# A hybrid attention step with a gathered expert layer on one core: the second head is chosen ahead of the first dot, query blocks take other ring places and come sooner, the late strips begin two slots later

## The chip, the core and the metric

The kernel runs on one core of a Trainium2 chip. The metric is the device time of one execution in microseconds, as the median of several runs. The engines are PE (TensorE), VectorE (DVE), ScalarE (ACT), GpSimd (POOL) and SyncE (SP); the core has 16 DMA engines, which all queues share.

## The reference

One layer of a decoder runs over 256 prompt tokens and 32 sample tokens (8 sequences of 4, each with 2048 cached positions). All is float32, the model width is 2048.

```python
h = layer_norm(ALPHA * x + mix @ w_out, ln1_g, ln1_b)           # mix: stick-breaking heads | sparse attention heads
return layer_norm(ALPHA * h + peer_ffn(h, ...), ln2_g, ln2_b)

# peer_ffn, for each block of tokens xc
q = (xc @ w_query).reshape(128, 8, 2, 128)
s = jnp.einsum('thcd,ckd->thck', q, sub_keys)
top_s, top_i = lax.top_k(s, 16)                                  # 16 best of 128 sub-keys, on both sides
cand_s, cand_i = 16 x 16 sums and expert numbers
best_s, best_j = lax.top_k(cand_s, 16)
experts = jnp.take_along_axis(cand_i, best_j, axis=-1)           # 8 heads x 16 experts for each token
gate = jax.nn.softmax(best_s, axis=-1)
act = jax.nn.gelu(jnp.einsum('thkd,td->thk', u_tab[experts], xc))
return jnp.einsum('thk,thkd->td', gate * act, v_tab[experts])
```

Ahead of it stand one input projection, stick-breaking attention over prompt and cache, and the sparse attention (compressed keys, selected blocks, a window) over prompt and cache.

## The kernel before, in words

**Stages.** The input projection and the attention of the prompt's early rows come first, with 1 MB blocks of weights and cache pages streamed through a ring. Then the output projection for the first 160 tokens (128 "full rows", tile 0, and 32 rows, tile 1), their layer norm, the query projection and the choice of experts. From there on a long loop of 288 slots gathers expert rows, while the attention of the samples and of the last prompt rows, with all that follows for the last 128 tokens, runs in the loop's background.

**The ring.** `Stream` (L276) numbers the 1 MB items that SyncE loads and gives each one of 8 ring places (`RING`, 8192 bytes a partition each). `room` is how many items must be used before a place is free again; PE raises `item_used` by one with the last matmul on each item. The 16 blocks of `w_out` ("output blocks", key `wo`) lie in places 4 to 7 and 0 to 3 in turn, twice; the 16 blocks of `w_query` ("query blocks", key `wq`) take place k modulo 4. Places 4 to 7 (`u_ring`) are left to the gathers of `peer_u`, places 0 to 3 (`v_ring`) go to those of `peer_v` once all items are used (`stream.n`).

**Order on PE** (L1588 to L1669). For output blocks 0 to 7 both tiles' passes follow block by block; for 8 to 15 the full rows of all eight come first, and only then the 32-row passes (`out_rows(k, 1)`), each of which ends its block's use. Then the first two query blocks' full rows (their use doesn't end there), the turned rows of tile 1, `query_parts` for blocks 0 to 2, which end their use, and blocks 3 to 15 (`query_rows`), one after another, each followed by the scores of the one before.

**Order on SyncE** (L687 to L729). The output blocks, `w1_one` (one side of the compression weights), the query blocks in order, then the background's items (`Background`): pages of the compressed caches in places of another set (`later_rows`, four areas of 2048 words from `AT_T` on, of which the first pages use the third and fourth). The page numbers are read into registers ahead of each set of pages. ScalarE issues the odd pages from the third set on.

**Order on VectorE** (L2746 to L2762). Rows of tile 0 and 1 are normed, then the first head of tile 0 is chosen: `head_part` 0 and 1 take the 16 best sub-keys on each side, part 2 the 16 best pairs; `first_ranks` and `second_ranks` make expert numbers, `fold` lays them out by slot. `chosen` tells GpSimd. Then comes the slot loop. A slot `s` runs `selection(s)` (parts of other heads by tables of slot numbers: `HEAD_PARTS`, `EXPERT_PARTS`, `EXPERT_HEADS`), `background(s)` and `gather_dot(s)`: it waits for gathered rows in ring place 4 + s % 4 and multiplies and sums 128 x 2048 values in one instruction.

**Order on GpSimd** (L2815 to L2859). It waits for the first `chosen` and for the ring, then issues in each step `s` the gather of `peer_u` for slot s (when the dot of slot s - 4 is done) and, from s = 19 on, that of `peer_v` for slot s - 19. `CHOSEN_BY` says which slots wait for a further head.

**Late strips.** Six units of the prompt's sparse attention (`LATE`) run in the loop. A unit that begins at slot or tick L has scores on PE at L, `strip_mask` on VectorE at L + 1, exponentials on ScalarE at L + 2, `strip_norm` at L + 3, PE's transposes at L + 4 (`LATE_TURN`), the values on PE at L + 5 (`LATE_PV`) and the result's copy at L + 6. `strip_cmp_in` copies the transposed compressed probabilities; VectorE runs it at the end of slot L + 4, and PE's values wait for it.

Of the kernel before, what the change touches and what calls it, by code (L numbers as in the profile page):

```python
# [145 lines left out]
RING = 8  # L146
# [11 lines left out]
LATE_AT, LATE_STEP = 14, 6  # L158
# [116 lines left out]

class Stream(Items):  # L276


    def __init__(self):
        super().__init__(RING)  # L280
        order = []
        for step, m in enumerate(ORDER):
            order.append((("w_in", m), 1))
            for name, at in (("ak", AK_AT), ("av", AV_AT)):
                if step in at:
                    order += [((name, at[step], b4), 2) for b4 in range(4)]
        order += [(("av", i, b4), 2) for i in range(8, 16) for b4 in range(4)]
        order += [(("wo", k), 1) for k in range(16)]
        for key, dmas in order:
            self.add(key, self.n % RING, dmas)  # L290
        for k in range(16):
            self.add(("wq", k), k % 4, 1)
# [71 lines left out]
def hybrid_step(nc, dram, outs):  # L364
    stream, later_items = Stream(), Background()
    with ExitStack() as ctx:
# [45 lines left out]
        ring = [words(AT_RING + 2048 * s, 2048) for s in range(RING)]  # L412
# [26 lines left out]
        ring_full = [sem(f"ring_full{s}") for s in range(RING)]  # L439
# [197 lines left out]
        HEAD_PARTS = {part: (0, 1, part) for part in range(3)}  # L637
        HEAD_PARTS.update({4 + 3 * k + part: (0, 2 + k, part) for k in range(2) for part in range(3)})
# [5 lines left out]
        EXPERT_PARTS = {10: (0, 1, 0), 11: (0, 1, 1), 27: (0, 2, 0), 28: (0, 2, 1), 43: (0, 3, 0), 44: (0, 3, 1)}  # L644
        EXPERT_PARTS.update({91 + 8 * p + part: (1, p, part) for p in range(4) for part in range(2)})
        EXPERT_PARTS.update({QUERY_AT + 10 + 12 * p + part: (2, p, part) for p in range(1, 4) for part in range(2)})
        EXPERT_HEADS = {3: (0, 1), QUERY_AT + 6: (2, 0), QUERY_AT + 10: (2, 1)}
# [24 lines left out]
        def _(sp):  # L672
# [40 lines left out]
            for k in range(16):  # L713
                load(("wq", k), dram["w_query"][k].rearrange("p k n -> p (k n)"))
# [17 lines left out]
            sp.wait_ge(h_in, 5)  # L732
            for kv in range(2):
# [1247 lines left out]
        def _(dve):  # L1981
# [497 lines left out]
            def experts_head(tt, h):  # L2479
                first_ranks(tt, h, 1)  # L2480
                second_ranks(tt, h, 1)
# [144 lines left out]
            def background(s):  # L2626
                if s in LATE_OUT:
                    strip_out(LATE_OUT[s])
                if s in LATE_MASK:
# [118 lines left out]
            experts_head(0, 0)  # L2748
            dve.wait_ge(saved, 1)

            for s in range(SLOTS_ALL):
                selection(s)
# [6 lines left out]
                if s in LATE_TURN:  # L2759
                    strip_cmp_in(LATE_TURN[s])  # L2760
# [20 lines left out]
        def _(pool):  # L2781
# [34 lines left out]
            pool.wait_ge(item_used, stream.used["wo", 15])  # L2816
# [95 lines left out]
```

## Time and profile before

| | before |
|---|---|
| median of 3 runs | 2444.26 us (2441.86 to 2447.72) |
| the profiled execution's own time | 2442.06 us |
| its span, first to last instruction | 2440.3 us |
| PE busy | 1744.5 us (71%) |
| VectorE busy | 1281.0 us (52%) |
| GpSimd busy | 842.5 us (35%) |
| moved by DMA | 961.28 MB, mean 394 GB/s |
| mean granted TensorE clock | 0.801 of full speed |

The span is what the profile's rows are about; the own time holds a little around it. Busy shares are means over stages with different limits. The page's second part shows the span in 40 slices of 61 us each, as tenths of busy time. The stretches and rows of single engines that matter lie between 586 and 760 us, at the turn from the output projection to the slot loop.

### The profile page before, as it was taken

To read this page: it belongs to the slowest core of one execution; us is meant where nothing else is said; L and a number is where in the kernel's file an instruction comes from. 1 tells how busy PE (TensorE), PEld (TensorE's weight loads), DVE (VectorE), ACT (ScalarE), POOL (GpSimd) and SP (SyncE) were. 2 spreads that over 40 slices of the span, in tenths; PEclk is the share of its full clock that TensorE was granted. 3 is DMA by queue.
4 is the path that set the end of the run, shared out by engine and by line. 5 is a ranking of instruction groups with operands and counts; after the bars stand their busy time and mean duration, and the time that the engine had idled before them with its cause. 6 is when DMAs were issued, how large, how long until landed. Compare 5 with 4: busy or idle time off the path is not lost.

```text
span 2440.3 us, 30172 instructions
## 1 busy us (share of the span) xinstructions
PE 1744.5 (71%) x9939; PEld 967.4 (40%) x9939; DVE 1281.0 (52%) x2454; ACT 354.1 (15%) x817; POOL 842.5 (35%) x595
## 2 busy tenths in 40 slices
PE   8999999989989877887565756869433333355335
PEld 6777766643887655565312222228100000000000
DVE  0600112362797877557958452245788754455651
ACT  0001101330411111111100020022200010021111
POOL 0000000000123434343323242242665677767662
PEclk9999999999999988889787878979555555555556
DMA  9989999998699999999999999999999999999998
GB/s 386 374 343 362 369 386 374 367 387 333 280 377 384 406 407 409 407 407 406 398 390 396 390 402 407 419 421 421 419 422 412 422 422 421 422 421 422 422 422 324
DMA packets 213309, 961.28 MB, mean 394 GB/s; under 512 B 23841, under 2 KB 89378, under 8 KB 122754
## 3 DMA queue, kind: packets, MB, share of 16 engines
q0 software_dynamic: 84432, 626.31, 62.4%
q1 hardware_dynamic: 92914, 300.39, 31.8%
q10 hardware_dynamic: 35808, 32.65, 4.0%
q8 instruction: 80, 1.31, 0.2%
q14 instruction: 75, 0.61, 0.1%
HBM read 952.77 MB, written 14.88 MB: 397 GB/s over the span
## 4 chain that ended last, share of the span: by engine, by line
DMA 43%; PE 41%; DVE 6%; ACTq 4%; issue 4%; POOL 1%; ACT 1%; SPq 0%; POOLq 0%; DVEq 0%
DMA sb<-in_peer_v,sb 23%; PE bank L1197 14%; DMA sb<-in_nsa_t 13%; PE bank L1677 6%; DMA sb<-in_peer_u,sb 4%; PE bank L1960 4%; PE bank L1563 3%; PE bank L1610 3%; PE bank L1268 2%; DVE sb L2706 2%; ACTq L455 2%; DMA sb<-in_nsa_v 2%; PE bank L1296 2%; ACTq L1034 1%; PE bank L1875 1%
## 5 line engine op out<-in xcount | busy, mean ns | idle before, releaser
L2706 DVE CUSTOM_DVE_ANT_0 sb<-sb 128x2048 f32<-128x2048 f32 x288 | 659.5, 2293 | 448.8 <-DMA sb<-in_peer_u,sb 443.4
L1960 PE MATMUL bank<-sb 128*32 128x512 f32 x2304 | 466.9, 861 | 495.8 <-DMA sb<-in_peer_v,sb 459.4
L2819 POOL DMA_INDIRECT sb<-in_peer_v,sb x288 | 503.9, 1749 | 525.3 <-PE bank L1960 476.5
L2819 POOL DMA_INDIRECT sb<-in_peer_u,sb x288 | 330.2, 1147 | 491.7 <-DVE sb L2706 287.8
L1960 PEld LDWEIGHTS bank<-sb 128*32 128x32 f32 x2304 | 60.8, 126 | 806.1 <-DMA sb<-in_peer_v,sb 730.0
L1197 PE MATMUL bank<-sb 128*128 128x288 f32 x1408 | 352.1, 410 | 7.7 <-DMA sb<-in_tokens_t 7.7
L1677 PE MATMUL bank<-sb 128*128 128x256 f32 x1024 | 275.3, 428 | 84.1 <-DMA sb<-in_nsa_t 72.1
L1197 PEld LDWEIGHTS bank<-sb 128*128 128x128 f32 x1408 | 266.1, 191 | 92.7 <-issue 13.9
L1677 PEld LDWEIGHTS bank<-sb 128*128 128x128 f32 x1024 | 247.0, 309 | 123.3 <-DMA sb<-in_nsa_t 85.1
L1154 ACT ACTIVATE sb<-sb 128x32 f32<-128x32 f32 x288 | 87.4, 316 | 720.1 <-PE bank L1960 433.9
L2803 POOL DMA_DIRECT2D out_a<-sb x1 | 0.5, 547 | 501.7 <-PE bank L1296 501.7
L1743 PE MATMUL bank<-sb 128*32 128x512 f32 x128 | 66.1, 692 | 43.0 <-DMA sb<-in_nsa_t 43.0
L1797 PE MATMUL bank<-sb 128*32 128x256 f32 x256 | 62.5, 426 | 30.7 <-DMA sb<-in_nsa_v 30.7
L779 ACT ACTIVATE sb<-bank 128x288 f32<-128x288 f32 x44 | 18.1, 411 | 410.1 <-PE bank L1197 410.1
L962 ACT ACTIVATE sb<-sb 32x2048 f32<-32x2048 f32 x36 | 68.6, 1906 | 39.7 <-issue 26.2
L1563 PE MATMUL bank<-sb 128*32 128x512 f32 (+1 forms) x256 | 71.8, 599 | 0.1
L1610 PE MATMUL bank<-sb 128*128 128x160 f32 (+1 forms) x512 | 71.0, 297 | 0.7 <-ACT sb L935 0.7
L1610 PEld LDWEIGHTS bank<-sb 128*128 128x128 f32 x512 | 67.7, 190 | 3.3 <-ACT sb L975 2.0
L1296 PE MATMUL bank<-sb 128*32 128x512 f32 x512 | 60.9, 597 | 5.1 <-DMA sb<-in_a_v 5.0
L1875 PE MATMUL bank<-sb 128*128 128x128 f32 x512 | 61.0, 279 | 3.4 <-DMA sb<-in_w_query 3.4
L1875 PEld LDWEIGHTS bank<-sb 128*128 128x128 f32 x512 | 58.7, 194 | 11.7 <-DMA sb<-in_w_query 7.5
L1268 PE MATMUL bank<-sb 128*32 128x256 f32 x1024 | 58.6, 380 | 0.0
(412 smaller groups left out, 1448.7 us busy)
## 6 DMA issues: line engine op xcount, KB each, us to landing
sb<-in_a_k SPq DMA_DIRECT2D x128, 512.0 KB, 7.3
sb<-in_a_v SPq DMA_DIRECT2D x128, 512.0 KB, 6.8
sb<-in_w_in SPq DMA_DIRECT2D x43, 1024.0 KB, 9.2
sb<-in_w_out SPq DMA_DIRECT2D x32, 1024.0 KB, 19.3
sb<-in_w_query SPq DMA_DIRECT2D x32, 1024.0 KB, 9.7
sb<-in_nsa_t SPq DMA_DIRECT2D x200, 128.0 KB
sb<-in_nsa_t ACTq DMA_DIRECT2D x184, 128.0 KB
sb<-in_nsa_v SPq DMA_DIRECT2D x64, 128.0 KB
```

Of the source, the lines that this page charges most:

```text
L962: act.activation(replica(g)[32 * q:32 * q + 32], src, ACT.Copy).then_inc(rep_in, 1)
L1154: act.activation(diag[j % 4], const["fold"], ACT.Copy, scale=w16[:, r % 2, j:j + 1]).then_inc(diag_in, 1)
L1197: mm = pe.matmul(bank[step % 2][:, 0:T], w[:, kt * P:(kt + 1) * P], x_t[:, kt, :], start=(kt == 0), stop=(kt == KT - 1))
L1268: mm = pe.matmul(bank[4 + u % 2][32 * b4:32 * b4 + 32, 256 * pp:256 * pp + 256], q_pad_a[:, half, b4, h], rows[b4][:, :, h, :], start=(h = ...
L1296: mm = pe.matmul(bank[(0 if half else 6) + c][r, :], z_t[:, half, 2 * pp + j, r], rows[b4][:, 1024 * j + 512 * c:1024 * j + 512 * c + 512] ...
L1563: mm = pe.matmul(bank[3 * (n % 2) + tt][own, :], mix(4 * kq + kt)[:, P * tt:P * tt + rows], w[:, kt, :], start=(kq == 0 and kt < parts), s ...
L1610: mm = pe.matmul(bank[5 if m == 1 else 1 if m == 2 else m % 2][:, 0:count], w[:, P * kt:P * kt + P], h_t[:, kt, 0:count], start=(kt == 0), ...
L1677: mm = pe.matmul(bank[(7, 3)[n % 2]][:, 0:256], rows[:, :, l], w1_one[:, :, l, :], start=(l == 0), stop=(l == 15), skip_group_check=True)
L1875: mm = pe.matmul(bank[2 + m % 2][:, 0:ROWS_2], w[:, P * kt:P * kt + P], h_t2[:, kt, :], start=(kt == 0), stop=(kt == KT - 1))
L1960: mm = pe.matmul(bank[g % 2][32 * c:32 * c + 32, :], diag[j % 4], rows[:, 512 * c:512 * c + 512], start=(s in FIRST), stop=(s in LAST), sk ...
L2706: dve.tensor_tensor_reduce(out=u, in0=u, in1=replica(g), scale=1.0, scalar=0.0, op0=ALU.mult, op1=ALU.add, accum_out=act16[:, r % 2, j:j + ...
L2819: pool.indirect_dma_start(rows[j % 4], None, dram[table], bass.IndirectOffsetOnAxis(ap=idx, axis=0)).then_inc(full[j % 4], 16)
```

## The change

- The set of ring places grows by a ninth, `words(AT_T + 4096, 2048)`. It is the area that the third set of the background's places uses later.
- Query blocks take places by a table: 0 to 2 in places 4 to 6, 3 to 6 in 0 to 3, block 7 in the ninth, then 0, 1, 2, 3, ninth, 0, 1, 2. SyncE issues block 7 ahead of block 0.
- Before the first pages SyncE waits until query block 12 is used. GpSimd waits for query block 2 in place of output block 15 before its first gather.
- The second head of tile 0 is chosen (three parts and its first ranks) ahead of the loop. Its second ranks and folds are at slot 1 in a new function. Heads 2 and 3 and the pair's expert numbers move two slots forward.
- The late strips begin at 16 in place of 14, and `strip_cmp_in` moves from the end of slot L + 4 to the background of slot L + 5.

```diff
-LATE_AT, LATE_STEP = 14, 6
+LATE_AT, LATE_STEP = 16, 6
+WQ_AT = (4, 5, 6, 0, 1, 2, 3, 8, 0, 1, 2, 3, 8, 0, 1, 2)
...
         for k in range(16):
-            self.add(("wq", k), k % 4, 1)
+            self.add(("wq", k), WQ_AT[k], 1)
...
-        ring = [words(AT_RING + 2048 * s, 2048) for s in range(RING)]
+        ring = [words(AT_RING + 2048 * s, 2048) for s in range(RING)] + [words(AT_T + 4096, 2048)]
...
-        HEAD_PARTS = {part: (0, 1, part) for part in range(3)}
-        HEAD_PARTS.update({4 + 3 * k + part: (0, 2 + k, part) for k in range(2) for part in range(3)})
+        HEAD_PARTS = {2 + 3 * k + part: (0, 2 + k, part) for k in range(2) for part in range(3)}
...
-        EXPERT_PARTS = {10: (0, 1, 0), 11: (0, 1, 1), 27: (0, 2, 0), 28: (0, 2, 1), 43: (0, 3, 0), 44: (0, 3, 1)}
+        EXPERT_PARTS = {8: (0, 1, 0), 9: (0, 1, 1), 27: (0, 2, 0), 28: (0, 2, 1), 43: (0, 3, 0), 44: (0, 3, 1)}
...
-        EXPERT_HEADS = {3: (0, 1), QUERY_AT + 6: (2, 0), QUERY_AT + 10: (2, 1)}
+        EXPERT_HEADS = {QUERY_AT + 6: (2, 0), QUERY_AT + 10: (2, 1)}
...
-            for k in range(16):
+            for k in (7, *range(7), *range(8, 16)):
                 load(("wq", k), dram["w_query"][k].rearrange("p k n -> p (k n)"))
...
             sp.wait_ge(h_in, 5)
+            sp.wait_ge(item_used, stream.used["wq", 12])
...
             def experts_head(tt, h):
                 first_ranks(tt, h, 1)
+                experts_told(tt, h)
+
+            def experts_told(tt, h):
                 second_ranks(tt, h, 1)
...
             def background(s):
                 if s in LATE_OUT:
                     strip_out(LATE_OUT[s])
+                if s in LATE_PV:
+                    strip_cmp_in(LATE_PV[s])
...
             experts_head(0, 0)
+            for part in range(3):
+                head_part(0, 1, part)
+            first_ranks(0, 1, 1)
             dve.wait_ge(saved, 1)

             for s in range(SLOTS_ALL):
+                if s == 1:
+                    experts_told(0, 1)
                 selection(s)
...
                 gather_dot(s)
-                if s in LATE_TURN:
-                    strip_cmp_in(LATE_TURN[s])
...
             pool.wait_ge(chosen, 1)
-            pool.wait_ge(item_used, stream.used["wo", 15])
+            pool.wait_ge(item_used, stream.used["wq", 2])
```

## Rows read from the trace of the kernel before

**Rows 1.** The page: mean busy share of the DMA engines, 40 slices, in tenths.

```profile
DMA  9989999998699999999999999999999999999998
```

**Rows 2.** Busy time by stretch: bounds and length, engines, granted clock, DMA share, GB/s.

```profile
598.00:619.00 21.00, 21.00 (x86) 8.38 (x88) 5.08 (x10) 2.30 (x3) 0.00 (x0) 1.00 0.01 4
619.00:630.00 11.00, 9.92 (x88) 7.90 (x81) 10.48 (x24) 4.26 (x6) 0.00 (x0) 1.00 0.95 379
630.00:640.00 10.00, 9.37 (x147) 8.84 (x149) 9.01 (x30) 6.29 (x12) 0.00 (x0) 1.00 0.09 14
640.00:646.00 6.00, 6.00 (x65) 5.80 (x58) 5.00 (x22) 2.88 (x4) 0.26 (x1) 1.00 0.91 365
646.00:714.00 68.00, 67.34 (x462) 62.74 (x463) 56.48 (x144) 22.46 (x49) 14.06 (x15) 1.00 1.02 413
714.00:719.00 5.00, 5.00 (x24) 5.00 (x24) 5.00 (x5) 0.38 (x1) 3.04 (x2) 1.00 0.30 80
768.00:775.00 7.00, 7.00 (x36) 5.93 (x35) 6.65 (x16) 0.38 (x1) 2.70 (x3) 1.00 0.88 297
720.00:1520.00 800.00, 575.51 (x2859) 361.56 (x2858) 536.83 (x1069) 102.36 (x283) 289.19 (x233) 0.85 1.03 401
1520.00:2400.00 880.00, 446.30 (x2424) 120.39 (x2424) 499.10 (x832) 119.09 (x268) 520.92 (x322) 0.60 1.01 419
```

**Rows 3.** SyncE's queue in order of time: start, length, line, what, number.

```profile
586.83 0.37 SPq L712 DMA_DIRECT2D sb<-in_cmp_w  x1
618.49 2.90 SPq L687 DMA_DIRECT2D sb<-in_w_query  x4
638.94 6.81 SPq L687 DMA_DIRECT2D sb<-in_w_query  x4
687.17 0.33 SPq L687 DMA_DIRECT2D sb<-in_w_query  x1
692.14 3.96 SPq L725 DMA_DIRECT2D sb<-in_nsa_t  x8
700.71 3.46 SPq L725 DMA_DIRECT2D sb<-in_nsa_t  x6
```

**Rows 4.** PE in order of time, and SyncE's waits from 598 to 720.

```profile
620.93 1.09 PE L1578 MATMUL bank<-sb 128*128 128x128 f32 x8
640.88 4.51 PE L1610 MATMUL bank<-sb 128*128 128x160 f32 x32
709.51 11.02 PE L1677 MATMUL bank<-sb 128*128 128x256 f32 x48 [0.66 <-ACT sb L967]
...
SPq L687 <- PE bank L1563: 32.8, 4, 31.3
```

**Rows 5.** VectorE in order of time; brackets: idle before, and its releaser.

```profile
614.10 0.69 DVE L2341 SCALAR_TENSOR_TENSOR sb<-sb,bank 128x512 f32<-128x512 f32 x1 [13.04 <-PE bank L1563]
633.00 0.30 DVE L2399 MAX8 sb<-sb 128x8 f32<-128x128 f32 x1
639.65 0.15 DVE L2422 COPY sb<-sb 128x1 f32<-128x1 f32 x1
642.48 0.43 DVE L2440 TENSOR_TENSOR sb<-sb 128x256 f32<-128x256 f32 x1
655.68 2.29 DVE L2706 CUSTOM_DVE_ANT_0 sb<-sb 128x2048 f32<-128x2048 f32 x1 [7.98 <-DMA sb<-in_peer_u,sb]
714.76 2.29 DVE L2706 CUSTOM_DVE_ANT_0 sb<-sb 128x2048 f32<-128x2048 f32 x1
751.38 0.28 DVE L2178 COPY sb<-bank 15x128 f32<-15x128 f32 x1 [8.18 <-PE bank L1396]
```

**Rows 6.** GpSimd in order of time.

```profile
645.74 1.00 POOL L2819 DMA_INDIRECT sb<-in_peer_u,sb  x1 [82.06 <-DVEq L2486]
715.65 2.21 POOL L2819 DMA_INDIRECT sb<-in_peer_u,sb  x1 [5.43 <-DVE sb L2706]
759.08 0.94 POOL L2819 DMA_INDIRECT sb<-in_peer_u,sb  x1 [12.59 <-DVE sb L2706]
```

More of the change, by code:

```diff
@@ L273, in add @@
         self.used[key] = self.n
+WQ_AT = (4, 5, 6, 0, 1, 2, 3, 8, 0, 1, 2, 3, 8, 0, 1, 2)
 class Stream(Items):
     def __init__(self):
-        super().__init__(RING)
+        super().__init__(RING + 1)
         order = []
@@ L438, in hybrid_step @@
         item_used = sem("item_used")
-        ring_full = [sem(f"ring_full{s}") for s in range(RING)]
+        ring_full = [sem(f"ring_full{s}") for s in range(RING + 1)]
         consts_in, first_in, x_in, wg_in, rope_in, w1_in, pages_in = (sem(n) for n in (
```

## The prediction

> **What bounds the kernel now.** I read the page first: the DMA row of its 40 slices is at 9 nearly everywhere and falls to 6 in one slice, the eleventh (610 to 671 us) [rows 1]. The reader is to see that a full row of DMA engines is the limit, and that the kernel gets shorter only where they stand still. So I went to the busy time by stretch for the DMA share [rows 2]. From 720 us on it is 1.01 over two long stretches, with one small dip (0.88 over 7 us at 768). Between 598 and 719 it has three holes. A: share 0.01 over 21 us and 0.95 over the next 11, together 20.8 + 0.5 = 21.3 us. B: 0.09 over 10 us and 0.91 over 6, together 9.1 + 0.5 = 9.6 us. C: 0.30 over 5 us, 3.5 us. With the dip D (0.12 x 7 = 0.8 us) that is 35.2 us. Both sides of the change read and write the same bytes, so the time gained is the idle time of the DMA engines taken away, less what is added.
>
> Then the queues around these holes. SyncE issues the slab of compression weights at 586.83, and next query block 0 at 618.49; blocks 4 to 7 go out from 638.94 [rows 3]. SyncE's waits put this down to PE's output-projection line, 31.3 us the longest: block 0 waits for the ring place of output block 12 [rows 4]. VectorE works without a gap from 614.10 to the end of the first head's selection; GpSimd's first gather is at 645.74, released by it [rows 5, 6]. One 1 MB item takes 1.0486 MB / 413 GB/s = 2.54 us of all engines, from the stretch 646 to 714 [rows 2].
>
> **Hole A.** Query block 7 gets a ring place of its own (behind the ring, where neither the slab of compression weights nor the norms lie), no wait, and is issued first, right behind 586.83: one item, 2.5 us, moves into the hole. Blocks 0 to 2 go to places 4 to 6, so block 0 waits for output block 8 instead of 12. The one-row passes of blocks 8 to 15 lie between VectorE's row at 614.10 (which the last full-row pass releases, some 0.2 us before) and PE's next line at 620.93: 7.0 us for eight, 0.88 each [rows 4, 5]. Four of them earlier is 3.5 us: issue at 618.49 - 3.5 = 615.0. The blocks behind it (places of blocks 12 to 15) are issued between 618.5 and 621.2 as now, while the first three keep the engines busy 7.6 us: no gap. A shrinks by 2.5 + 3.5 = 6.0 us.
>
> **Hole B.** Seven blocks (0 to 6) then run from about 615.9 (the issue and the 0.9 us that the engines took after 618.49 to be busy in the stretches) to 615.9 + 7 x 2.54 = 633.7. The next work is block 8, which waits for block 3's place (now the fourth issue of the row at 638.94, about 645.4), and the first gather. Neither comes earlier: VectorE's chain from 614.10 has no wait on the moved transfers, it ends at 645.7 as now, and GpSimd's new wait (query block 2 used, instead of output block 15) is met before 640.88, when PE is past those parts [rows 4]. So the engines stand from 633.7 to about 646.4: 12.7 us instead of 9.6, 3.1 us lost. If the first gather or block 8 came 1 us later, B grows by 1 us. A and B together give 2.9 us.
>
> **The first slots.** Now VectorE waits 7.98 us for the first gathered rows, until 655.68, since they queue with blocks 4 to 7 [rows 5]. After, the queue is empty at 645.7, so the rows land within two or three items (some 5 to 7 us), by about 652. What takes VectorE's wait in exchange is its own work: the second head's three parts and its first ranks are put there. From the first head's rows, 633.00 to 639.65 is 6.65 us and to 642.48 another 2.83, together 9.5 us [rows 5], so the first dot starts at 645.7 + 9.5 = 655.2 instead of 655.7: which costs nothing. Slots 0 to 3 are rid of 6.65 + 2.83 us less the first part (about 1.8): 7.7 us of lead. The rest of that head (3.2 us: 642.48 to 645.7) stays, at slot 1. The pair's ranks move from slots 10, 11 to 8, 9, behind heads 2 and 3, which begin two slots sooner.
>
> **Hole C.** It is there because no gather is out: GpSimd idles 5.43 us before 715.65, for a dot that stands behind the pair's ranks at slot 11, and the page loads wait for PE's taps at 709.51 (released at 717) [rows 4, 6]. With the lead, the dot of slot 11 ends near 707.5, and five dots of 2.29 us follow one another [rows 5]: the gathers 15 to 18 come between 707 and 715. The ledger from 646.4: 8 query blocks, gathers 0 to 14 and 2 MB of pages are 25 items, 63.5 us, to 709.9; gathers 15 to 18 to 720; by then the next pages (717.2 as now) and gather 19 with the first value gather are there. C goes: +3.5 us. Worth between 0 (hole moved, not closed) and 3.5; I take 3.5 because each demand in the ledger is issued before its turn.
>
> **The waits on SyncE.** The first page load now waits for query block 12 used. PE's blocks of 5.1 us (640.88 to 709.51 less the scores' end, 13 blocks) make that 640.9 + 10 x 5.1 = 692; today the last query block goes out at 687.17 and, after eight page numbers are read, the first page at 692.14 [rows 3]. So the first pages start at 692 + 5.0 = 697, the second set at 705.5 instead of 700.71, done issuing near 710. Behind the waiting instruction stand only these pages. PE wants the first set at 709.51 and the second at half of its 11 us row, near 717: the first set has 8 us after its last issue, the second 7, for 2 to 3 items. Cost 0; if the margin fails, its lower bound is 0 and its upper the 4.8 us shift itself.
>
> **The late strips.** The strips start at slots 16, 22, ... instead of 14, 20, ..., and the copy of the turned probabilities moves from the end of a slot to the next one, behind its selection. Today that copy makes VectorE wait 8.18 us (751.38), GpSimd has no gather for 12.59 us, and the dip D, 0.8 us, follows [rows 2, 5, 6]. Moving it can return 0.8. Against it: the mask of the first strip now waits for scores that stand on PE behind the third set of pages' taps, so VectorE may wait at slot 17 instead. Bounds: +0.8 and, one such stall with two gathers (5.1 us) out, about -4. I take 0, nearest to D's row. The strips' ends at slot 52 have the output projection far behind them.
>
> **A rule weighed.** The gather issued at 715.65 took 2.21 us where others took 1.00 [rows 6]; the dot that began at 714.76 ended at 717.05, the next came at once [rows 5]. The Trainium skill, "SBUF — State Buffer", section "Who interferes with whom", says that a VectorE instruction with two inputs in SBUF and a GpSimd instruction that reads SBUF exclude each other, the loser blocked for the whole instruction. By that rule, the trace agrees. It speaks against this change, since it makes five dots in a row where the gathers are needed; its time is the third case below, worked out from the rows.
>
> **Sum.** 6.0 - 3.1 + 3.5 + 0 = 6.4 us. The profiled execution took 2442.06 us, its span 2440.3: 2442.06 - 6.4 = 2435.7. The median is 2.2 above the profiled one, and a median is what is forecast: 2444.26 - 6.4 = **2437.9 us**. A difference under 0.2% (4.9 us: below 2439.4, above 2449.1) can't be told from none.
>
> **Cases.**
> 1. As summed, 2437.9, own range 2434 to 2441: chance 0.50, of which 0.06 lies within 0.2%.
> 2. Only A and B count: the lead in dots is spent, since slot 16 waits for PE's turn at 725 anyway, and hole C comes back between 722 and 745. Gain 2.9, 2441.4. For it: PE's chain to 709.51 is untouched; against: the value gathers can start with slot 15. Chance 0.20, nearly all within 0.2%.
> 3. Gathers shut out by dots: one gather per dot, each a dot late. The first of the row then misses its turn by 2.3 us: 2440.2. Chance 0.08, within.
> 4. The strips' move also returns D, and waits for the strips elsewhere in VectorE's first 50 slots shorten: gain 7.2 to 10, 2435.5. Chance 0.10, faster.
> 5. Slower: the strips' waits. At slot 17 the mask, and again at the next unit, and the one after, holds VectorE as long as the copy did (8.2 us), now with only 5.1 us of gathers out. Each empties the queue for about 5 us (8.2 and a slot's own 2.3 less 5.1); three are 15 lost against 6.4: 2444.3 + 8.6 = 2452.9. It makes the kernel slower from the second stall on, and measurably from the third. For it: one stall of 8.18 is there now; against: it cost but 0.8. Chance 0.12.
>
> Faster by over 0.2%: 0.44 + 0.10 + 0.03 of case 2 = 0.57; within: 0.06 + 0.17 + 0.08 = 0.31; slower: 0.12. The range goes from case 4's better end, 2434.3, less the 2.4 us by which a run shown lies under the median, to 2446, one hole of case 5 beyond case 1 and the scatter (2437.9 + 5 + 3).
>
> **What would show it.** Query block 0 issued near 615, one block right behind 586.8; DMA idle from about 601 to 616 and 634 to 646, and a share of 1 from 646 through 725; first dot near 655; slot 11's dot over before 709; first pages at 697; PE's taps still at 709.5. Wrong if: the first gather comes later than 646.5, a hole of over 2 us opens between 690 and 760, VectorE waits over 8 us at a strip's mask, or PE waits for the first pages.

## The result and the profile after

| | before | after |
|---|---|---|
| median on one chip, 11 runs each | 2445.17 us (2441.86 to 2448.36) | 2451.53 us (2447.3 to 2455.63) |
| ratio after / before | | 1.0020, 95% interval 1.0011 to 1.0029 |
| the profiled execution, own time and span | 2442.06 and 2440.3 us | 2449.86 and 2448.1 us |
| mean granted TensorE clock | 0.801 | 0.795 |

The change makes the kernel slower by 0.2% (0.0020 of 2445.17 is 4.9 us; the plain medians lie 6.4 apart). Forecast were 2437.9 us and a gain of 6.4.

After, busy time by stretch, in the columns of [rows 2] (length; PE, PEld, VectorE, ScalarE and GpSimd busy; granted clock; DMA share; GB/s):

```profile
598.00:619.00 21.00, 21.00 (x83) 8.42 (x85) 4.68 (x10) 2.30 (x3) 0.00 (x0) 1.00 0.25 97
619.00:630.00 11.00, 9.92 (x88) 7.63 (x81) 10.52 (x23) 4.18 (x6) 0.00 (x0) 1.00 0.99 416
630.00:640.00 10.00, 9.37 (x138) 8.84 (x141) 9.05 (x29) 6.29 (x13) 0.00 (x0) 1.00 0.47 195
640.00:646.00 6.00, 6.00 (x79) 5.80 (x67) 5.15 (x23) 2.83 (x5) 0.00 (x0) 1.00 0.00 0
646.00:714.00 68.00, 67.34 (x464) 62.76 (x464) 62.06 (x150) 22.57 (x50) 19.85 (x18) 1.00 0.96 381
714.00:719.00 5.00, 3.39 (x16) 3.09 (x14) 3.96 (x11) 0.38 (x1) 1.62 (x2) 1.00 1.02 415
733.00:747.00 14.00, 13.53 (x66) 13.18 (x66) 5.71 (x15) 0.98 (x3) 1.87 (x2) 1.00 0.39 110
720.00:1520.00 800.00, 583.84 (x2842) 366.21 (x2843) 524.22 (x1044) 101.23 (x279) 289.80 (x227) 0.84 1.01 394
```

A is 21 x 0.75 + 11 x 0.01 = 15.9 us (forecast 15.3, before 21.3). B is 10 x 0.53 + 6 = 11.3 us (forecast 12.7, before 9.6). C is full: 1.02 where [rows 2] has 0.30. But two things stand where nothing was forecast. One is a new hole, 0.39 from 733 to 747, 8.5 us. The other is the stretch from 646 to 714, at 0.96 after 1.02 of [rows 2]. In parts, with 1.02, 1.02 and 1.05 for the same three before:

```profile
646.00:660.00 14.00, 14.00 (x101) 12.99 (x101) 12.76 (x45) 8.27 (x14) 5.01 (x5) 1.00 0.93 376
690.00:703.00 13.00, 13.00 (x94) 12.24 (x93) 12.04 (x31) 1.81 (x7) 2.00 (x2) 1.00 0.92 350
703.00:709.00 6.00, 6.00 (x43) 5.36 (x42) 6.00 (x5) 1.47 (x6) 4.82 (x3) 1.00 0.76 242
```

One us each is missing right behind the first gather and from 690 to 703 (the pages start at 697 and not at 692), and 1.4 us from 703 to 709. The view of the DMA queues from 702 to 710, 40 slices of 0.2 us, shows the last one:

```profile
DMA  8979999999999910000000993663989898999959
```

The engines are dry from 705.0 to 706.4: it is hole C, 10 us sooner and less than half as long. GpSimd's gather beside the dots in a row takes 2.21 us there, as in [rows 6] (703.57 below).

SyncE's queue after, as [rows 3]:

```profile
587.23 0.37 SPq L714 DMA_DIRECT2D sb<-in_cmp_w  x1
...
697.30 4.30 SPq L727 DMA_DIRECT2D sb<-in_nsa_t  x8
706.20 3.94 SPq L727 DMA_DIRECT2D sb<-in_nsa_t  x8
```

The two sets of pages are issued where the prediction put them (697 and 705.5, done near 710). PE after, in order of time, as [rows 4]. These matmuls multiply the pages with the compression weights (the prediction's "taps"), 32 for each set of 8 pages; brackets hold the idle time before:

```profile
709.92 7.47 PE L1680 MATMUL bank<-sb 128*128 128x256 f32 x32 [0.66 <-ACT sb L970]
727.44 6.00 PE L1680 MATMUL bank<-sb 128*128 128x256 f32 x16 [10.05 <-DMA sb<-in_nsa_t]
```

This is the failure. Before, the row at 709.51 has 48 matmuls without a stop. Now PE does the first set's 32 and stands 10.05 us for the second set, whose last issue ended at 706.20 + 3.94 = 710.14: 17 us from last issue to use. VectorE and GpSimd after, as [rows 5, 6]; dots stand for rows between:

```profile
655.68 2.29 DVE L2714 CUSTOM_DVE_ANT_0 sb<-sb 128x2048 f32<-128x2048 f32 x1
...
738.83 0.48 DVE L2527 TENSOR_SCALAR sb<-bank,sb 128x256 f32<-128x256 f32 x1 [16.50 <-PE bank L1692]
```

```profile
646.13 0.99 POOL L2830 DMA_INDIRECT sb<-in_peer_u,sb  x1 [82.22 <-DVEq L2492]
...
703.57 2.21 POOL L2830 DMA_INDIRECT sb<-in_peer_u,sb  x1 [5.43 <-DVE sb L2714]
...
710.51 0.94 POOL L2830 DMA_INDIRECT sb<-in_peer_u,sb  x1 [0.30 <-issue]
...
743.70 0.94 POOL L2830 DMA_INDIRECT sb<-in_peer_u,sb  x1 [19.01 <-DVE sb L2714]
```

Read these as a chain. The gathers have their lead: the one of slot 16 comes at 710.51, and in the kernel before at 718.17, 7.66 us later (forecast were 7.7 us of lead). Then VectorE waits 16.50 us for PE's taps, no dot runs, no ring place comes free, and GpSimd issues nothing for 19.01 us. The DMA engines have nothing left, and the hole at 733 opens.

### The profile page after: what moved, and what is told of

It is laid out like the page before. It is cut to its first block, busy times and chain, and to the rows that moved or that the text cites. A ratio compares the mean times of both kernels' runs of the same rounds, so it can differ in the third digit from the quotient of the medians.

```text
span 2448.1 us, 30172 instructions
## 1 busy us (share of the span) xinstructions
PE 1756.8 (72%) x9939; PEld 971.4 (40%) x9939; DVE 1280.5 (52%) x2454; ACT 353.9 (14%) x817; POOL 851.8 (35%) x595
## 4 chain that ended last, share of the span: by engine, by line
DMA 43%; PE 38%; DVE 7%; issue 5%; ACTq 3%; POOL 1%; SPq 1%; ACT 1%; POOLq 0%; DVEq 0%
DMA sb<-in_peer_v,sb 25%; PE bank L1200 14%; DMA sb<-in_nsa_t 9%; DMA sb<-in_peer_u,sb 5%; PE bank L1680 4%; PE bank L1963 4%; PE bank L1566 3%; DVE sb L2714 3%; PE bank L1271 2%; PE bank L1613 2%; DMA sb<-in_nsa_v 2%; PE bank L1299 2%; ACTq L458 2%; POOL sb L2830 1%; DMA sb<-in_w_out 1%
## 5 line engine op out<-in xcount | busy, mean ns | idle before, releaser
L1963 PE MATMUL bank<-sb 128*32 128x512 f32 x2304 | 468.7, 862 | 485.3 <-DMA sb<-in_peer_v,sb 455.5
L2830 POOL DMA_INDIRECT sb<-in_peer_u,sb x288 | 340.6, 1183 | 488.9 <-DVE sb L2714 284.5
L1746 PE MATMUL bank<-sb 128*32 128x512 f32 x128 | 70.7, 738 | 42.7 <-DMA sb<-in_nsa_t 42.7
L1800 PE MATMUL bank<-sb 128*32 128x256 f32 x256 | 63.6, 435 | 32.4 <-DMA sb<-in_nsa_v 32.4
L1299 PE MATMUL bank<-sb 128*32 128x512 f32 x512 | 60.9, 598 | 5.3 <-DMA sb<-in_a_v 5.3
L1839 PE MATMUL bank<-sb 128*32 128x512 f32 x512 | 59.3, 608 | 4.0 <-DMA sb<-in_w_out 4.0
```

The source lines that it names most:

```text
L1299: mm = pe.matmul(bank[(0 if half else 6) + c][r, :], z_t[:, half, 2 * pp + j, r], rows[b4][:, 1024 * j + 512 * c:1024 * j + 512 * c + 512] ...
L1746: mm = pe.matmul(bank[((5, 6), (7, 2))[ph][c]][32 * b4:32 * b4 + 32, :], q_pad[:, 4 * h + b4, g], rows[:, 4 * c:4 * c + 4, g, :], start=(g ...
L1963: mm = pe.matmul(bank[g % 2][32 * c:32 * c + 32, :], diag[j % 4], rows[:, 512 * c:512 * c + 512], start=(s in FIRST), stop=(s in LAST), sk ...
L2830: pool.indirect_dma_start(rows[j % 4], None, dram[table], bass.IndirectOffsetOnAxis(ap=idx, axis=0)).then_inc(full[j % 4], 16)
```

## Why the pages were late: packets, not items

The view of the DMA queues by stretch gives the packets, MB and share of each queue: q0 is GpSimd's (gathers), q1 SyncE's, q10 ScalarE's. Before, from 706 to 709:

```profile
q1 hardware_dynamic: 626, 0.57, 57.7%
q0 software_dynamic: 76, 0.62, 51.6%
```

After, from 715 to 718 and from 727 to 730:

```profile
q0 software_dynamic: 150, 1.10, 88.0%
q1 hardware_dynamic: 148, 0.14, 13.3%
...
q0 software_dynamic: 117, 0.96, 78.3%
q1 hardware_dynamic: 120, 0.11, 11.2%
q10 hardware_dynamic: 117, 0.11, 10.3%
```

From 715 to 718, where both queues have work, each moves the same number of packets (150 and 148), and with three queues too (117, 120, 117). A gather's packets are 7.3 KB in the mean (1.10 MB / 150), a page's 0.9 KB (0.14 MB / 148); the rows are 8 and 1 KB, and the count holds some packets under 512 B. So a page queue beside waiting gathers gets 1/9 of the bytes, 0.14 MB in 3 us, and a set of 1 MB would take 22 us. Before, GpSimd idled 5.22 us for want of a dot just ahead of this gather, and 5.43 us ahead of the next [rows 6]:

```profile
709.15 1.07 POOL L2819 DMA_INDIRECT sb<-in_peer_u,sb  x1 [5.22 <-DVE sb L2706]
```

So few gathers were out, 76 of their packets went by from 706 to 709, and the pages got 0.57 MB in these 3 us. Hole C itself let no page through: the second set's last packets moved by 713, and the view by queue has none of SyncE's from 713 to 718. What let the pages through were the same pauses of GpSimd for want of a dot of which hole C is the last. The Trainium skill, "DMA: Bandwidth & Descriptors", section "Queues, rings and completion order", says that each DMA engine goes round the queues that have work and changes only at a packet's end. By that rule, the trace agrees: 150 against 148.

## Experiments

Each was run beside the kernel before on the same chip, but not all on one chip; the kernel before had medians of 2445.72, 2446.71, 2445.82 and 2446.59 us beside them. So kernels are compared by their ratios to it, given with a 95% interval, and not by their medians.

| kernel | median, us | ratio | interval |
|---|---|---|---|
| strips_old | 2452.79 | 1.0028 | 1.0016 to 1.0039 |
| the changed kernel | 2451.53 | 1.0020 | 1.0011 to 1.0029 |
| head_wait_b | 2448.86 | 1.0010 | 0.9998 to 1.0023 |
| gathers_held | 2448.75 | 1.0009 | 0.9998 to 1.0019 |
| strips_only | 2445.85 | 0.9997 | 0.9988 to 1.0007 |
| split_pages_b | 2443.66 | 0.9997 | 0.9983 to 1.0012 |
| ring_once | 2445.22 | 0.9995 | 0.9985 to 1.0004 |
| before_wait | 2446.25 | 0.9994 | 0.9983 to 1.0005 |
| ring_wait_b | 2443.83 | 0.9993 | 0.9982 to 1.0003 |
| ninth_once | 2445.37 | 0.9989 | 0.9978 to 1.0000 |
| head_only | 2444.19 | 0.9988 | 0.9978 to 0.9998 |
| split_same_time | 2441.33 | 0.9984 | 0.9973 to 0.9995 |
| ninth_strips_old | 2442.00 | 0.9983 | 0.9973 to 0.9992 |
| scores_first_b | 2440.27 | 0.9975 | 0.9962 to 0.9988 |
| scores_split | 2440.39 | 0.9974 | 0.9965 to 0.9984 |

**ninth_once: the changed kernel, the ninth place used once, so that SyncE waits for block 7 only.**

```diff
-WQ_AT = (4, 5, 6, 0, 1, 2, 3, 8, 0, 1, 2, 3, 8, 0, 1, 2)
+WQ_AT = (4, 5, 6, 0, 1, 2, 3, 8, 0, 1, 2, 3, 0, 1, 2, 3)
-            sp.wait_ge(item_used, stream.used["wq", 12])
+            sp.wait_ge(item_used, stream.used["wq", 7])
```

> The changed kernel, with the ninth place used for query block 7 alone (places 4, 5, 6, 0, 1, 2, 3, 9th, 0, 1, 2, 3, 0, 1, 2, 3), so that SyncE waits for block 7 in place of block 12 and the first pages are issued near 692 again, as in the kernel before (697.30 in the changed one). Theory 1 (the second set of pages, issued at 706.2, shared the DMA engines packet by packet with a burst of gathers, 1 KB against 8 KB, landed 17 us after its last issue, and PE's wait of 10.05 us for it stopped VectorE for 16.50 us and GpSimd for 19.01): the sets are issued before the burst, PE waits under 2 us for pages between 709 and 730, the DMA hole from 733 to 747 (about 8 us idle) is gone, and the median falls by 7 to 10 us under the changed kernel, to 2441 to 2445. Theory 2 (the move of the late strips, with the other waits only following from it): no change beyond 2 us, 2450 to 2453. Theory 3 (the gathers' lead itself is what PE pays for, whenever pages are issued): PE still waits over 5 us, 2448 or more.

The pages start at 693.19, and the loss is gone: 0.9989 against 1.0020, apart by 0.0031 (with the two half-widths of the intervals taken together, 0.0009 and 0.0011, by 0.0017 to 0.0045). One thing more comes with this edit: with the ninth place used once, the last query block waits for a later place, and SyncE issues its last one at about 688 and not at 682. So head_wait_b below, where the wait stands without the ring's part, is needed too. The second set is in time, the third isn't:

```profile
732.93 9.36 PE L1680 MATMUL bank<-sb 128*128 128x256 f32 x32 [6.12 <-DMA sb<-in_nsa_t]
```

**strips_old: the changed kernel, with the late strips as before.**

```diff
-LATE_AT, LATE_STEP = 16, 6
+LATE_AT, LATE_STEP = 14, 6
-                if s in LATE_PV:
-                    strip_cmp_in(LATE_PV[s])
+                if s in LATE_TURN:
+                    strip_cmp_in(LATE_TURN[s])
```

> The changed kernel with the late strips alone put back: first at slot 14, and the copy of the turned probabilities at the end of slot L + 4. Theory 1 (late pages): the hole from 733 to 747 stays, PE's wait for pages at 717 to 727 stays near 10 us, the median stays within 3 us of the changed kernel's 2451.5, on either side, since the first strip's scores come ahead of the wait and its copy may stop VectorE again. Theory 2 (the strips' move is the loss): the median falls by 6 us or more, to 2445 or less.

It takes nothing of the loss away (1.0028). PE waits 6.56 us for the second set, VectorE 16.4 at the first mask, GpSimd 21.86: the strips' move isn't the cause, and with late pages the old order is no better.

**before_wait: the kernel before with SyncE's wait for query block 12 alone.**

```diff
             sp.wait_ge(h_in, 5)
+            sp.wait_ge(item_used, stream.used["wq", 12])
```

> The kernel before with one line added: SyncE waits until query block 12 is used before the first pages. Theory 1: the first pages are issued 5 us later (697 in place of 692), the second set at 706. VectorE is where it was, so the gathers 15 to 18 come only from 715 on, and hole C (share 0.30 from 714 to 719) is there for the pages: they land by about 718, PE waits 0 to 3 us for them, and the median is 0 to 3 us above 2445.2. A theory that the wait alone is the loss: PE waits about 5 us or more and the median is 5 us or more above.

0.9994: pages 4 us later cost nothing by themselves. The first starts at 696.09; PE waits 2.65 and 2.97 us where [rows 4] stands.

**gathers_held: the changed kernel; GpSimd waits for the second set before the gather of slot 15.**

```diff
             (GpSimd's loop)
+                if s == 15:
+                    pool.wait_ge(later_full[3], 128)
```

> The changed kernel with one wait more on GpSimd: gather 15 and those behind it are held until the second set of pages has landed. If pages and gathers share the engines by packets (theory 1), the set that is issued by 710 lands by about 713 instead of 727, PE's wait at 717 is gone, VectorE's 16.50 us at the sums are gone, and the DMA hole at 733 to 747 with them, against a hole of up to 3 us near 710 and dots a few us later: median 4 to 8 us under the changed kernel, 2443 to 2448. If the set was late for its own issue or for a slow path of its own, it lands no earlier than 720 and the median stays at 2451 or above.

With the gathers out of the way the second set lands by 716.7, 10 us sooner, and PE's row has its 48 matmuls again. Its PE and GpSimd:

```profile
710.00 11.02 PE L1680 MATMUL bank<-sb 128*128 128x256 f32 x48 [0.66 <-ACT sb L970]
```

```profile
716.74 0.94 POOL L2830 DMA_INDIRECT sb<-in_peer_u,sb  x1 [8.62 <-DVE sb L2714]
751.93 0.94 POOL L2830 DMA_INDIRECT sb<-in_peer_u,sb  x1 [18.44 <-DVE sb L2714]
```

So gathers are what delays the pages. But the third set then meets the gathers: PE waits 9.60 us for it at 735.90, VectorE 14.86 us at the mask, and GpSimd's gap (18.44) is as long as in the changed kernel (19.01), only later. The hole was expected to go and the median to reach 2443 to 2448; neither came. How much of the loss stays isn't told: 1.0009 is clearly apart neither from the changed kernel nor from the one before.

**ninth_strips_old: ninth_once and strips_old together.** Its diff is the two above.

> The changed kernel with the ninth place used once (block 7) and the late strips back at 14 with the old copy: the first two parts of the change alone, with early pages. With the ninth place used once, PE still waited 6.12 us for the third set of pages, and VectorE 10.46 us at the first strip's mask, whose scores stand behind that set's taps. Theory 1 (each wait is for pages behind gathers, and the mask only passes it on): with scores at 14 the mask is not stopped, VectorE waits under 3 us there, though some of it comes back at the copy of slot 18; the median is 1 to 4 us under that kernel's 2445.4, 2441.5 to 2444.5. Theory 2 (the strips' place is neutral here too, since the whole is bound by DMA afterwards): within 1 us, 2444.5 to 2446.5.

0.9983, faster than the kernel before. From ninth_once it can't be told (0.9989); here the mask waits 7.55 us and GpSimd 12.59.

**ring_once, head_only, strips_only: the kernel before with one part of the change each** (ring and query blocks with the ninth place used once, SyncE's order of blocks and GpSimd's wait as changed; the second head's choice ahead of the first dot, with the tables of slots as changed; the strips' move). Each is shortened to its main lines:

```diff
ring_once:   +WQ_AT = (4, 5, 6, 0, 1, 2, 3, 8, 0, 1, 2, 3, 0, 1, 2, 3)
             +sp.wait_ge(item_used, stream.used["wq", 7])
head_only:   +head_part(0, 1, 0..2); first_ranks(0, 1, 1)   ahead of the slot loop
strips_only: -LATE_AT = 14   +LATE_AT = 16, strip_cmp_in in background(L + 5)
```

> The kernel before with the places and the order of the query blocks alone (the ninth place used once, pages issued near 692). Holes A and B by the prediction's sum are 2.9 us less. Theory 1 (a lead of the dots over PE's pages is given back in waits): the first gathered rows land early, VectorE's wait of 7.98 us shrinks to about 3 us, its dots are 4 to 5 us ahead, and the burst of gathers falls on the second and third set; the gain of 2.9 is kept in part, 2443 to 2446. A theory that the ring part is simply good and the head the spoiler: 2440 to 2443.

> The kernel before with the second head chosen ahead of the first dot and heads 2, 3 and the pair two slots earlier, nothing else. The first gathered rows land at 655.7 as before, and the head takes 9.5 us from 645.7, so the first dot is at 655.7; the dots lead by 7 to 8 us at slot 16 as in the changed kernel, and gathers 14 to 18 come between 703 and 715, while pages are issued at 692 and 700. Theory 1: pages of the third set wait behind the gathers, hole C (3.5 us) closes at 714 but one of 3 to 5 us opens between 733 and 750; median 2444 to 2448. If a lead of the dots is worth what it closes: 2441 to 2443.

> The kernel before with the late strips two slots later and the copy in the next slot, nothing else. Theory 1 (the strips only pass on waits for pages): VectorE's wait of 8.18 us at the copy goes, a wait of 2 to 8 us comes at the first mask (slot 17), the dip of 0.8 us at 768 goes; median within 2 us of 2445.7. Theory 2 (the strips are the loss): 5 us or more above.

The head's move is worth a little alone (0.9988), the ring's part and the strips' can't be told from nothing. In head_only the first dot is at 657.59, since the gathers queue with query blocks; in ring_once it is at 654.84, 6.19 us waited. In head_wait_b below, whose code is the same as head_only's up to there, it is at 655.90 with no wait, so these small waits differ between executions, and the ring's part isn't needed for a start without one.

strips_only missed its expectation on the waits (2 to 8 us at the first mask): its mask waits 13.52 us, PE 9.19 us for the third set, and GpSimd has a gap of 17.11 us, nearly that of the changed kernel. Its ratio is 0.9997 all the same. So a long gap in one profile doesn't by itself show a loss in the median. The profiled execution was the slowest of its eleven (2448.87 us).

**head_wait_b and ring_wait_b: the wait for block 12 with the head's move, and with the ring's part.**

```diff
head_wait_b: head_only   +sp.wait_ge(item_used, stream.used["wq", 12])
ring_wait_b: ring_once   -WQ_AT = (..., 8, 0, 1, 2, 3, 0, 1, 2, 3)
                         +WQ_AT = (..., 8, 0, 1, 2, 3, 8, 0, 1, 2)
                         -sp.wait_ge(item_used, stream.used["wq", 7])
                         +sp.wait_ge(item_used, stream.used["wq", 12])
```

> The kernel before with two things alone: the second head chosen ahead of the first dot, and SyncE's wait for query block 12 ahead of the pages. Ring and strips as before. Theory, that the loss comes from the two together (gathers come earlier, pages later, and pages asked for behind gathers get about a ninth of the bytes): the second set of pages lands late, TensorE waits 5 to 10 us for it at the taps, VectorE behind it, and GpSimd has a gap of over 14 us between 720 and 760; median 3 to 8 us above that of the head move alone, which was 2444.2, so 2447 to 2452. Rival, that the ring's part is needed too: no more than 2 us above the head move alone, 2443 to 2446.

> The kernel before with the ring's part alone, exactly as changed (ninth place used twice, so SyncE's wait for block 12 stands ahead of the pages); head and strips as before. Theory, that wait and lead must meet: the first dot stays near 655, the gathers have no lead, so the pages meet fewer gathers; median within 3 us of the ring part with the ninth place used once (2445.2), 2443 to 2448. Rival, that this wait costs the 5 us by which it shifts the pages wherever it stands: 2449 to 2452.

Both medians came out as the theory had it, though the first only just told apart. The wait alone is 0.9994, the head alone 0.9988, so side by side they would be 0.9982; together they are 1.0010, 0.0028 more (half-widths of 0.0011, 0.0010 and 0.0012 together: 0.0009 to 0.0047). With the ring's part the same wait is 0.9993, no loss. In head_wait_b PE waits for the second set and GpSimd behind it:

```profile
721.80 6.05 PE L1680 MATMUL bank<-sb 128*128 128x256 f32 x16 [4.30 <-DMA sb<-in_nsa_t]
```

```profile
737.67 0.93 POOL L2830 DMA_INDIRECT sb<-in_peer_u,sb  x1 [16.60 <-DVE sb L2712]
```

The wait of 4.30 us is a little under the 5 to 10 expected.

**split_pages_b: the changed kernel, the second set's odd pages in ScalarE's queue.**

```diff
             (SyncE)
-                                range(8) if kv == 0 and i < 2 else range(0, 8, 2))
+                                range(8) if kv == 0 and i < 1 else range(0, 8, 2))
             (ScalarE, in its loop over the query blocks)
+                if m == 13:
+                    act.wait_ge(pages_in, 16)
+                    for j in range(1, 8, 2):
+                        act.dma_start(later_rows[3][:, 256 * j:256 * j + 256], ...page 8 + j...)
```

> The changed kernel, and of the second set of pages the odd ones issued by ScalarE instead of SyncE, so that they stand in two queues; SyncE's wait is kept. Theory, that the DMA engines share by queue and packet, so that a page queue of 1 KB packets gets a ninth beside gathers of 8 KB: two queues get twice that, the second set lands some 4 us or more sooner (TensorE's wait of 10.05 us at its second half of the taps falls to below 6), and the median falls below the changed kernel's 2451.5, to 2447 to 2450. Rival, that the set is late by the time of its issue alone or that bytes in all are what limits: TensorE's wait stays within 1.5 us of 10.05 and the median at 2451 to 2453.

PE's wait of 10.05 us is gone entirely. But ScalarE's four pages went out at 700.32, 6 us ahead of those they replace, so a second queue and an early start are mixed here; and the interval is wide. Hence the next.

**split_same_time: the same with `m == 14`.**

> The kernel of split_pages_b with ScalarE's four pages issued one query block later. There ScalarE's four came at 700.3, 6 us sooner than the changed kernel's second set (706.2), so an early start and a second queue were mixed; TensorE's wait of 10.05 us was gone. Here they should be issued at about 705.4 to 709, no sooner than in the changed kernel. Theory, that a second queue is what counts (each gets a turn per packet beside the gathers): the set lands by 721, TensorE's wait for its second half falls to below 4 us, median within 3 us of 2443.7. Rival, that the early start did it: TensorE waits 7 us or more, median 2448 to 2452.

ScalarE issues at 704.95, SyncE its four at 704.77, where the changed kernel has 706.20: still 1.3 to 1.4 us sooner (half as many page numbers to read), and done at 708.6 in place of 710.1. PE, and then the queues from 712 to 715:

```profile
710.54 11.02 PE L1685 MATMUL bank<-sb 128*128 128x256 f32 x48 [0.66 <-ACT sb L970]
```

```profile
q0 software_dynamic: 149, 1.12, 90.1%
q10 hardware_dynamic: 149, 0.13, 13.1%
q1 hardware_dynamic: 35, 0.03, 2.6%
```

Again equal packets (149 and 149), SyncE's half is just ending, and ScalarE's ends in the next 3 us with 9 packets. From 709 to 712 the two queues brought 0.54 MB of pages, where the changed kernel's one brought 0.40. The ratio is 0.9984: 0.0036 below the changed kernel (0.0022 to 0.0050 with both half-widths), with SyncE's wait, the ring, the head and the strips all as changed. The rival had 7 us of wait and at least 2448; the numbers are the theory's. But how much of it is the second queue and how much the 1.3 us isn't separated: by 709 this kernel had moved 369 of the set's 1152 packets, a third of it, the changed one none. What the run does show is the cause of the loss: with the second set in time, and all else as changed, the loss is gone.

The Trainium skill, "DMA: Bandwidth & Descriptors", section "Issuing engines are not separate DMA queues", says that starting transfers on several engines only saves the time of their issue, since all run on the same DMA engines. For all bytes together that agrees (a DMA share of 1.02 in the changed kernel and of 1.03 in this one from 714 to 733). The share of one stream is another thing. In the changed kernel pages in one queue beside gathers got 0.14 MB in 3 us (715 to 718), and pages in two queues 0.22 MB (727 to 730).

**scores_first_b: ninth_strips_old, and PE's scores of the first strip ahead of the last 16 taps of set two.**

```diff
             (PE's ticks)
-                if t in LATE:
+                if t == 11:
+                    late_scores(EARLY_UNITS)
+                if t in LATE and t > LATE_AT:
```

> The changed kernel with the ninth place used once (SyncE waits for block 7 only), the strips at their old slots, and TensorE's scores of the first late strip put ahead of the third set's taps instead of behind them. Theory, that what is left of the stall at the first mask (7.55 us with the strips old and the ninth place once, which gave 2442.0) is TensorE's order: the mask's wait falls below 2 us, GpSimd's gap after it from 12.6 to below 6, and the median to 2438 to 2441. Rival, that the gathers' gap only moves to the copy of the turned probabilities, which waits for TensorE behind the third set: 2441 to 2444.

VectorE at the mask and at the copy of the turned probabilities:

```profile
717.49 0.23 DVE L2162 TENSOR_TENSOR bank<-bank,sb 128x64 f32<-128x64 f32 x1
...
744.00 0.28 DVE L2183 COPY sb<-bank 15x128 f32<-15x128 f32 x1 [5.29 <-PE bank L1399]
```

The mask's wait is 0 (7.55 before it). Both theories had a part: the median came as the first said, and part of the gap moved to the copy as the rival said (VectorE 5.29 us; GpSimd 6.33 us at 730.84, and 9.71 at 751.71). 0.9975 is faster than the kernel before and the changed one; from ninth_strips_old (0.9983) it can't be told.

**scores_split: scores_first_b with the second set split as in split_pages_b.**

> The kernel of scores_first_b with the second set's odd pages issued by ScalarE at query block 13 as in split_pages_b. Theory, that late pages are what still holds gathers back: GpSimd's gaps of 6.33 and 5.07 us between 720 and 735 shrink and the median falls by 1 to 2 us from 2440.3, to 2438 to 2439.5. Rival, that the second set is in time there already and the third set and the copy of the turned probabilities decide: the same within 1 us, 2439.5 to 2441.5.

2440.39 against 2440.27: nothing more. The second set is in time there already, as the rival said.

**One account for all.** What every one of these kernels moved from 598 to 775 us, against its profiled span (the GB/s of that stretch times 177 us). For the kernel before and the changed one:

```profile
598.00:775.00 177.00, 162.55 (x1054) 136.73 (x1053) 131.97 (x329) 43.96 (x95) 35.74 (x33) 0.96 0.81 318
```

```profile
598.00:775.00 177.00, 160.59 (x1041) 133.73 (x1040) 130.92 (x323) 44.65 (x98) 37.69 (x33) 0.96 0.79 308
```

| kernel | GB/s | MB by 775 | span, us |
|---|---|---|---|
| strips_old | 306 | 54.2 | 2448.7 |
| changed | 308 | 54.5 | 2448.1 |
| gathers_held | 309 | 54.7 | 2447.7 |
| strips_only | 311 | 55.0 | 2447.1 |
| head_wait_b | 312 | 55.2 | 2446.4 |
| ring_once, head_only | 318 | 56.3 | 2443.3, 2443.7 |
| before | 318 | 56.3 | 2440.3 |
| ninth_once, ring_wait_b | 320 | 56.6 | 2443.1, 2441.5 |
| split_pages_b, before_wait | 325 | 57.5 | 2438.2, 2437.3 |
| ninth_strips_old | 326 | 57.7 | 2439.3 |
| scores_first_b | 327 | 57.9 | 2438.8 |
| scores_split | 329 | 58.2 | 2443.6 |
| split_same_time | 331 | 58.6 | 2438.2 |

From 54.2 to 57.9 MB the span falls by 9.9 us, 2.7 us for each MB; a MB at 400 GB/s is 2.5 us. Before and before_wait stand some 3 us below this line and scores_split some 6 above. Each span is one execution, and executions of one kernel differ by more (the kernel before took 2440.8 to 2454.7 us on one chip). A row tells what that execution had lost by 775, and not what its kernel is worth: strips_only's profiled execution is its slowest, before_wait's its fastest (2439.13, median 2446.25). Within an execution the sum over bytes, the prediction's own measure, fits.

## Why the prediction was wrong, step by step

- **What bounds the kernel**: right, see the account above. Its "1.01 over two long stretches" is 1.03 and 1.01 in [rows 2]; nothing in the sum hangs on it.
- **Hole A**, +6.0: measured 21.3 - 15.9 = 5.4. Right.
- **Hole B**, -3.1: measured 9.6 - 11.3 = -1.7. The sign was right, the first gather is at 646.13, inside the bound of 646.5, and 1.0 us more is missing behind 646 (0.93), so -2.7. A and B together gave 2.7 of the 2.9; ring_once, where they stand alone, isn't told from nothing (0.9995).
- **The first slots**: right within 0.5 us for the first dot (655.2 forecast, 655.68 measured, no wait). The gathers of slots 15 to 18 came at 708.29, 710.51, 713.75 and 717.86 (forecast between 707 and 715; the last is 3 us out), so slot 11's dot was over by 708, as said.
- **Hole C**, +3.5: it went, as said (1.02). The chosen value failed even so, since it was counted as kept. "Worth between 0 (hole moved, not closed) and 3.5": the truth was below this range. 1.4 us of it moved with the lead to 705, and a larger one, 8.5 us, opened at 733.
- **The waits on SyncE**, cost 0: this is the step that failed. The times of issue were right within 0.7 us. What failed is "the first set has 8 us after its last issue, the second 7, for 2 to 3 items": the ledger let 1 MB items go in order of issue, but the DMA engines take packets in turn, so a set of pages behind gathers takes about 20 us. The bound "its upper the 4.8 us shift itself" failed too: PE waited 10.05, VectorE 16.50, GpSimd 19.01. In the whole the wait cost 0.0031 of 2445, 7.6 us (changed kernel less ninth_once). With the head's move as the only other part it cost 0.0022, 5.4 us (head_wait_b less head_only), and alone nothing (before_wait).
- **The late strips**, 0: right as far as the runs tell. The dip D is gone (a share of 1.02 from 768 to 775), as case 4 had it, and nothing came of it. Case 5, the forecast's way to slower, has nearly the time (2452.9 against 2451.53) but not the cause: its mask waits 2.2 us in the changed kernel, and strips_old keeps the loss. Where its mask does wait, 13.52 us in strips_only, the ratio is 0.9997.
- **The rule weighed** (gathers beside dots): the gather beside a dot took 2.21 us again, two more 1.90 and 1.91, and here the queue was dry behind it for 1.4 us. Case 3 put this at 2.3 us: right in kind, and small.
- **The two together.** Lead in gathers and delay of pages, each alone in the kernel before, cost nothing or bring 0.1% (head_only 0.9988, before_wait 0.9994). The loss is in both together: 0.0028, 6.8 us, beyond what each costs alone. No case of the prediction set the lead in gathers against the delay of pages. With the pages in time the same kernel is 0.2% faster than before (split_same_time, 0.9984, 3.9 us against the forecast 6.4), so the rest of the sum held in the main.
- **The signs of being wrong**: of the four named, one came true, a hole of over 2 us between 690 and 760. VectorE's long wait was at the sums of the pages and not at a mask, and PE's was for the second set and not for the first.

**What stays open.** By 775 us the changed kernel is 1.8 MB behind, 4.4 us of the 7.8 between the two profiled spans. From 1180 to 1520 us it moves 390 GB/s and the kernel before 396 (340 x 6 is 2.0 MB, 5 us), which is more than the other 3.4; from 1520 to 2400 it moves 420 against 419 and gets about 2 us back. But scores_first_b and split_same_time move 391 there and end sooner all the same. What lowers the rate there wasn't tried. Whether pages of larger packets would have been in time wasn't tried either, nor a second queue with an issue as late as the changed kernel's.

## What to carry to other kernels

A transfer's place in time isn't its place in the order of issue once another queue has work. Price it by packets: read in the view by queue how many packets and bytes each queue moves in a stretch where both are busy, and divide what is asked for by the small-packet queue's share. When idle time of the DMA engines is closed with big-packet traffic, look for who used that idle time: a stream of small packets with a deadline needs to be issued ahead of the big stream (ninth_once), or in more queues and somewhat sooner (split_same_time). Holding the big stream back at one deadline moved the wait to the next (gathers_held); holding it back at each wasn't tried.

## What the runs showed of the hardware

- Queues that all had work moved nearly equal numbers of packets, though of unlike size: 150 and 148, 149 and 149, 117 and 120 and 117 in 3 us each. Where the gathers' queue ran dry in between they didn't: 626 of the pages beside 76. With packets of 7.3 and 0.9 KB the bytes stand 8 to 1.
- TensorE's granted clock over 714 to 733 was 0.73 in the changed kernel, where PE idled 10.05 us, 0.89 in the kernel before, and 1.00 in scores_first_b, where PE waited 0.93 us there. Behind the stall of 10.05 us the matmuls were slower: from 727 to 733.3 the granted clock was 0.60 of full speed, so mostly at the lower of its two levels, and 16 matmuls took 6.00 us. At 733.72, at the full clock, 16 took 3.81.
- A gather by GpSimd that began during a dot on VectorE took longer and ended 0.8 us after that dot: 703.57 took 2.21 us (the dot ended at 704.97), 706.09 took 1.90 (707.19), 708.29 took 1.91 (709.40). The one at 710.51, ahead of the next dot at 710.64, took 0.94.
